# Twelve late conditioning slabs in the waits of three norms, a rebuilt LayerNorm, and the decay's low-rank product over column groups

## The chip, the cores and the metric

The kernel runs on one core of a Trainium2 chip. Its engines work side by side, each through its own program in order, and wait for one another on semaphores: TensorE (PE for its matmuls, PEld for its weight loads), VectorE (DVE), ScalarE (ACT), GpSimd (POOL) and SyncE (SP). POOL, SP and ACT also issue DMA transfers. The metric is the device time of one execution in microseconds (us); less is better.

## The reference, cut to what matters

One step of a one-layer decoder for 512 prompt tokens and 8 sampled tokens, 520 columns in all, width 1024.

```
mod = silu(c) @ w_ada + b_ada        # 9 x 1024, and 2 x 1024 of w_ada_final
h = rms_norm(x) * (1 + sc1) + sh1;   x = x + 0.5 * gt1 * swiglu(h)            # FFN1
h = rms_norm(x) * (1 + sc2) + sh2;   z = h @ w_in                             # the mixer
ca, cb, q, k, v, r, a_lr, g_conv, g_gla = split(z)
d = depthwise_conv(ca * sigmoid(cb));  y_conv = silu(layer_norm(d)) @ w_conv_out
log_a = log_sigmoid(a_lr @ w_alpha + b_alpha) / 16                            # rank 16
o = gla(q, k, v, log_a);               y_gla = (rms_norm(o) * silu(r)) @ w_gla_out
x = x + gt2 * ((sigmoid(g_conv) * y_conv + sigmoid(g_gla) * y_gla) @ w_out)
h = rms_norm(x) * (1 + sc3) + sh3;   x = x + 0.5 * gt3 * swiglu(h)            # FFN2
y = rms_norm(x) * (1 + scf) + shf
```

## The kernel before

Activations lie feature-major: eight tiles `t` of 128 features by 520 columns. Every weight product is cut into **units**, each 128 output features, numbered through the program by `plan()`. A unit (`unit`, L548) is 48 matmuls: eight k-tiles, three products (`w_hi*h_hi`, `w_hi*h_lo`, `w_lo*h_hi`), two halves of 260 columns. SP loads raw weights for two units (1 MB) into one of two slots of `raw`; ACT casts them to `w_hi` (L962), DVE subtracts for `w_lo` (L1322). Both are done in `step(n)`, once unit n is done, for unit n + 2. Even units write PSUM `pu0`, odd ones `pu1`, and a unit waits until its bank was read (`s_evac`). `unit_pair` (L564) runs two units side by side, k-tile by k-tile, as the tiles of h arrive.

**Conditioning slabs.** `w_ada` and `w_ada_final` are read in 44 slabs of 256 columns. A slab is eight fp32 matmuls with a 32-column stationary operand `c_f`, four of them in different column groups of the array (`ada_rows_of`, L581), then a copy of the rows by ACT (`ada_rows`, L985), two transposes with `sel` (`ada_transpose`, L592) and an add by DVE (`ada_out`, L1359). Slabs 0 to 7 stand at the start, 8 to 41 in pairs between the units of FFN1, 42 and 43 after it. FFN1 and FFN2 have the same 68 units, in three groups of up and down.

**A norm** (`norm_sums`, `rstd`, `modulate`): the squares of eight tiles are added up on DVE, PE sums over features with `ones` (L599), ACT takes Ln and Exp, DVE refines the root and multiplies, ACT modulates and casts, DVE subtracts for `h_lo` (L1468).

**Low rank of the decay** (`alr`, L1133): one whole unit whose first 16 output rows are used; its plan numbers stand for four units, and ACT and DVE pass two of them by counting semaphores.

**LayerNorm of the convolution** (L903 to L918): mean by PE, `centered` tiles (L1851), squares by ACT (L996) added up by DVE (L1380), `norm_sums(2)`, `o_sums` (L918) of heads 0 and 1 before the first unit of `yconv` and of heads 2 and 3 before its third (all single units); `o_roots`, `o_rstd`, and the gating of `o` (L1908 to L1913) go between the units of `yconv`. The units `ygla` read `o_hi` and `o_lo`.

Of the kernel before, what the change touches and what calls it, by code (L numbers as in the profile page):

```python
# [1968 lines left out]
```

## Time and profile before

| | |
|---|---|
| median of 3 runs | 1552.81 us (1550.1 to 1555.76) |
| the profiled execution | 1552.72 us, its span 1551.1 us |
| granted clock of TensorE, mean | 0.966 |
| FFN1, from its first unit to its last | 30.3 to 470.9 us |
| norm, then convolution, q and k, v | 470.9 to 700 us |
| gates and the linear attention | 700 to 952 us |
| LayerNorm, `yconv`, `ygla`, `out` | 952 to 1128 us |
| norm, FFN2, last norm | 1128 to 1551 us |

The profile is that of one execution; its time outside the span is 1.6 us. In the rows further on a start is in us from the start of the span, `x16` counts records (an fp32 matmul leaves two, an fp32r one), and `[5.03 <-DVE h_lo L1468]` says that the engine had been idle for 5.03 us until that instruction of DVE released it. Granted clock 1.00 is 2.4 GHz, 0.50 is 1.2 GHz.

### The profile page before, as it was taken

The numbers are of one execution on the slowest core, as the hardware profiler recorded it, in microseconds if no ns is written. First come the engines' busy times: TensorE is split into PE (matmuls) and PEld (weight loads), VectorE is DVE, ScalarE is ACT, GpSimd is POOL, SyncE is SP. The second block draws the span as 40 slices with busy tenths as digits, with TensorE's granted clock in tenths as the row PEclk, the third lists the DMA queues.
The fourth block names the chain that finished last, engine by engine and source line by source line (L and its number), as shares of the span: only waits on it lengthen the run. The fifth ranks groups of instructions, "written<-read, shape, count | busy, mean of one in ns | idle before, by whom it ended". The sixth has DMA issues, their size and how long they took to land. (4 is left out here: it accounts for less than half of the span.)

```text
span 1551.1 us, 30240 instructions
## 1 busy us (share of the span) xinstructions
PE 1451.4 (94%) x11934; PEld 1399.7 (90%) x11934; DVE 825.3 (53%) x1381; ACT 487.0 (31%) x660; POOL 73.5 (5%) x108
## 2 busy tenths in 40 slices
PE   6999999999997998999998895899979999999996
PEld 5899999999997998998998895799979999999995
DVE  5323322332256685798795977775453343333345
ACT  5322122212235223433232233522252212222233
POOL 6100000000010000000000000000000000000000
PEclk9999999999999999999898998899989999999997
DMA  9754545454554223222323333322312322322311
GB/s 311 235 168 154 172 152 173 147 178 142 170 189 147 84 81 113 72 93 79 130 93 122 105 123 132 137 83 88 103 55 82 104 85 82 108 82 84 99 61 55
DMA packets 134277, 189.03 MB, mean 122 GB/s; under 512 B 3516, under 2 KB 114512, under 8 KB 134159
## 3 DMA queue, kind: packets, MB, share of 16 engines
q1 hardware_dynamic: 113436, 114.57, 23.3%
q0 software_dynamic: 16704, 64.75, 12.5%
q10 hardware_dynamic: 4050, 8.53, 1.5%
q8 instruction: 58, 0.95, 0.3%
q14 instruction: 29, 0.23, 0.0%
HBM read 174.37 MB, written 14.41 MB: 122 GB/s over the span
## 5 line engine op out<-in xcount | busy, mean ns | idle before, releaser
L1322 DVE TENSOR_TENSOR w_lo<-raw,w_hi 128x1024 fp32r<-128x1024 f32 x218 | 266.8, 1225 | 589.6 <-ACT w_hi L962 589.4
L548 PE MATMUL pu<-h_hi,w_hi 128*128 128x260 f32 x2480 | 508.1, 286 | 19.4 <-DVE w_lo L1322 10.5
L548 PE MATMUL pu<-h_hi,w_lo 128*128 128x260 f32 x2480 | 501.5, 284 | 0.0
L548 PE MATMUL pu<-h_lo,w_hi 128*128 128x260 f32 x2480 | 500.8, 284 | 0.0
L962 ACT CAST w_hi<-raw 128x1024 fp32r<-128x1024 f32 x218 | 227.9, 1046 | 682.3 <-PE pu L548 670.6
L548 PEld LDWEIGHTS pu<-h_hi,w_hi 128*128 128x128 f32 x2480 | 384.5, 190 | 27.5 <-issue 10.9
L548 PEld LDWEIGHTS pu<-h_lo,w_hi 128*128 128x128 f32 x2480 | 384.4, 190 | 0.0
L548 PEld LDWEIGHTS pu<-h_hi,w_lo 128*128 128x128 f32 x2480 | 384.3, 189 | 0.0
L1617 DVE SCALAR_TENSOR_TENSOR d<-u,cw,d 128x512 f32<-128x512 f32 x240 | 162.9, 747 | 0.0
L548 PE MATMUL pu<-f_hi,w_hi 128*128 128x260 f32 x704 | 143.0, 284 | 2.0 <-DVE f_lo L1571 2.0
L548 PE MATMUL pu<-f_hi,w_lo 128*128 128x260 f32 x704 | 141.8, 283 | 0.0
L548 PE MATMUL pu<-f_lo,w_hi 128*128 128x260 f32 x704 | 141.3, 282 | 0.0
L548 PEld LDWEIGHTS pu<-f_hi,w_hi 128*128 128x128 f32 x704 | 108.3, 188 | 4.9 <-issue 2.5
L548 PEld LDWEIGHTS pu<-f_hi,w_lo 128*128 128x128 f32 x704 | 108.4, 188 | 0.0
L548 PEld LDWEIGHTS pu<-f_lo,w_hi 128*128 128x128 f32 x704 | 108.3, 188 | 0.0
L1088 ACT CAST f_hi<-sg 128x520 f32 (+1 forms) x44 | 27.6, 627 | 87.8 <-DVE sg L1568 87.8
L1571 DVE TENSOR_TENSOR f_lo<-sg,f_hi 128x520 f32 (+1 forms) x44 | 30.8, 701 | 40.4 <-ACT f_hi L1088 40.4
L581 PE MATMUL pg<-raw_a,c_f 128*32 128x256 f32 x640 | 38.9, 382 | 1.1 <-DMA raw_a<-in_w_ada 1.1
L1207 ACT ACTIVATE work<-work 128x512 f32<-128x512 f32 x28 | 17.7, 632 | 68.2 <-DVE work L1724 68.0
L418 POOL DMA_DIRECT2D raw_a<-in_w_ada x28 | 24.6, 884 | 297.6 <-PE pg L581 296.8
L811 PEld LDWEIGHTS pg<-work 128*128 128x128 f32 x224 | 28.0, 196 | 8.6 <-DVE work L1743 4.4
L811 PE MATMUL pg<-work 128*128 128x128 f32 x224 | 31.4, 287 | 3.2 <-DVE work L1743 3.2
(260 smaller groups left out, 1242.3 us busy)
## 6 DMA issues: line engine op xcount, KB each, us to landing
raw_a<-in_w_ada POOLq DMA_DIRECT2D x32, 1024.0 KB, 7.8
raw<-in_w_in SPq DMA_DIRECT2D x30, 1024.0 KB, 5.3
raw<-in_ffn_up SPq DMA_DIRECT2D x22, 1024.0 KB, 5.3
raw<-in_ffn_gate SPq DMA_DIRECT2D x21, 1024.0 KB, 5.3
raw<-in_ffn_down SPq DMA_DIRECT2D x16, 1024.0 KB, 5.1
raw_a<-in_w_ada_final POOLq DMA_DIRECT2D x8, 1024.0 KB, 7.4
gates_d<-sg ACTq DMA_DIRECT2D x24, 260.0 KB, 2.0
raw<-in_ffn_down SPq DMA_DIRECT2D x8, 768.0 KB, 4.5
```

The source lines that it names most:

```text
L418: pool.dma_start(dst, v[:, :, bass.ds(c, 256)]).then_inc(s_loaded, 16)
L548: last = mm(pu[p][:, e, 0:HALF], w[p][:, k, :], m[:, k, e * HALF:(e + 1) * HALF], start=(k == 0 and j == 0), stop=(k == k_tiles - 1 and j ...
L581: last = mm(pg[CG * g:CG * (g + 1), 2 + slot, 0:256], c_f[:, k, :], src[:, k, :], start=(k < 4), stop=(k >= 4), tile_position=(0, CG * g))
L811: last = mm(pg[:, l % 2, c * CH:(c + 1) * CH], m, m if rhs is None else rhs[:, c * CH:(c + 1) * CH], start=True, stop=True)
L962: nc.scalar.copy(w_hi[p][:], raw[:, slot, :, p * P:(p + 1) * P]).then_inc(s_hi, 1)
L1088: nc.scalar.copy(tile(f_hi, Lin(2 * k0 + c - 2, 2, i).value()), sg[:, c - 2, :]).then_inc(s_ahi, 1)
L1207: af(E_[:, l % 2, :], E_[:, l % 2, :], ACT.Exp, scale=1 / 16).then_inc(s_ge, 1)
L1322: V.tensor_tensor(w_lo[p][:], raw[:, slot, :, p * P:(p + 1) * P], w_hi[p][:].bitcast(F32), ALU.subtract).then_inc(s_lo, 1)
L1571: V.tensor_tensor(tile(f_lo, t.value()), s, tile(f_hi, t.value()).bitcast(F32), ALU.subtract).then_inc(s_a, 1)
L1617: conv.mark(V.scalar_tensor_tensor(d[:, t, 0:NP], flat(u[:, t:t + 1, bass.ds(tap + s, NP)]), cw[:, bass.ds((tap + s) * KT + t, 1)], d[:, t ...
```

## The change

1. **Slabs.** Slabs 32 to 43 leave FFN1 and the place behind it. Four each stand in the norm before the mixer, in the LayerNorm, and in the norm before FFN2 (`late_slabs`), two to a PSUM bank, with one copy of 512 columns for two slabs (`late_rows`), eight transposes for four (`late_transposes`) and one add (`late_out`). Their loads, issued by POOL, go to the memory that `LATE` names.
2. **LayerNorm.** PE sums each tile's squares itself; DVE no longer adds them up. The mean's sum no longer waits for `s_oe`. The first head's sums and root stand before `yconv`, whose first two units are now a `unit_pair`; the other heads follow between the units. `refine_d` replaces `refine`.
3. **Decay's low rank.** `alr` is gone from the plan. `a_rows` multiplies h by `wa` (16 columns of `w_in`, padded to 32) in column groups, into PSUM bank `pg`; `walpha` holds its 16 rows four times, 128 partitions with zeros between, so that the next product adds up the groups.

```diff
+LATE0 = 32
+LATE_BANK = [0, 2, 0]
-                        + [("conv", 16), ("alr", 4), ("qk", 8), ("v", 8), ("gates", 24),
+                        + [("conv", 16), ("qk", 8), ("v", 8), ("gates", 24),
...
+        LATE = [((raw_a, "a1"), (raw_q, "q")), ((raw_v, "v2"), (raw_h, "h")), ((raw_a, "a3"), (raw_v, "v3"))]
...
             ffn(1)
+            sp.wait_ge(s_wz, 1)
+            sp.dma_start(wa[:, :, 0:RANK], w_in[:, W_IN["a"]:W_IN["a"] + RANK].rearrange("(k p) n -> p k n", p=P)
+                         ).then_inc(s_wa, 16)
...
-            pair(Lin(at["alr"]), w_in, W_IN["a"], (w_in, W_IN["a"]))
...
+            late_load(0, 1)
+            pool.wait_ge(s_ad, LATE0)
+            late_load(0, 0)
...
+                if h + 1 == HEADS:
+                    pool.wait_ge(s_gk, HEADS)
+                    late_load(1, 0)
                 pool.wait_ge(s_oe, 2 * h + 1)
                 pool.dma_start(st_out[h], ST).then_inc(s_sto, 16)
+                if h + 1 == HEADS:
+                    pool.wait_ge(s_done, at["yconv"])
+                    late_load(1, 1)
...
+            pool.wait_ge(s_done, at["out"])
+            late_load(2, 0)
+            late_load(2, 1)
...
+            def late_slabs(stage):
+                for two in range(2):
+                    src, name = LATE[stage][two]
+                    pe.wait_ge(s_late[name], 32)
+                    for j in range(2):
+                        last = slab_rows(src[:, j], 2 + two, 256 * j)
+                    last.then_inc(s_lb, 1)
...
-            ada(Lin(ADA_SLABS - 2))
-            ada(Lin(ADA_SLABS - 1))
+            pe.wait_ge(s_ar, LATE0)
+            late_slabs(0)
...
-            pe.wait_ge(s_evac[1], n // 2)
-            unit(Lin(n), 0, h_hi, h_lo, done=4)
+            def a_rows():
+                pe.wait_ge(s_wa, 16)
+                pe.wait_ge(s_cve, KT)
+                for r in range(2):
+                    for j, m in enumerate((h_hi, h_lo)):
+                        for e in range(2):
+                            for g in range(4):
+                                last = mm(pg[CG * g:CG * (g + 1), 2 + e, 0:HALF], wa[:, 4 * r + g, :],
+                                          m[:, 4 * r + g, e * HALF:(e + 1) * HALF].bitcast(F32), start=(r == 0 and j == 0),
+                                          stop=(r == 1 and j == 1), tile_position=(0, CG * g))
+                last.then_inc(s_ao, 1)
...
             pe.wait_ge(s_ln, 2)
+            sums(sg[:, 2, :]).then_inc(s_ss, 1)
             pe.wait_ge(s_oe, 2 * HEADS)
-            sums(sg[:, 2, :]).then_inc(s_ss, 1)
-            norm_sums(2)
+            late_slabs(1)
+            for t in range(KT):
+                pe.wait_ge(s_sq, KT + t + 1)
+                sums(sg[:, t % 3, :], start=(t == 0), stop=(t == KT - 1)).then_inc(s_sqf, 1)
...
+            pe.wait_ge(s_lr, 4)
+            o_sums(0)
+            unit_pair(Lin(at["yconv"]), h_hi, h_lo, s_h, 2 * KT)
+            o_sums(1)
+            late_transposes(1)
+            for c in range(2, 4):
+                unit(Lin(at["yconv"] + c), c % 2, h_hi, h_lo)
+                o_sums(c)
...
             norm_sums(3)
+            pe.wait_ge(s_or, HEADS)
+            late_slabs(2)
...
-            rstd(4, SILU)
+            rstd(3, SILU)
+            late_rows(2, 0)
             modulate(3, SC3, SH3)
+            late_rows(2, 1)
...
             modulate(3, SC3, SH3)
+            late_out(2)
```

TensorE's program between the last unit of the convolution (fed by `h_hi`, `h_lo`, L548 before and L580 after) and the transposes of `u`; first of before, the first rows of `alr` only:

```order
L548 MATMUL pu<-h_lo,w_hi 128x260 x2
L548 MATMUL pu<-h_hi,w_lo 128x260 x2
L114 REGISTER_ALU
L114 COMPARE_AND_BRANCH
L548 MATMUL pu<-h_hi,w_hi 128x260 x2
L548 MATMUL pu<-h_lo,w_hi 128x260 x2
L548 MATMUL pu<-h_hi,w_lo 128x260 x2
L548 MATMUL pu<-h_hi,w_hi 128x260 x2
```

and after:

```order
L580 MATMUL pu<-h_lo,w_hi 128x260 x2
L580 MATMUL pu<-h_hi,w_lo 128x260 x2
L114 REGISTER_ALU
L114 COMPARE_AND_BRANCH
L814 MATMUL pg<-h_hi,wa 32x260 x8
L814 MATMUL pg<-h_lo,wa 32x260 x8
L814 MATMUL pg<-h_hi,wa 32x260 x8
L814 MATMUL pg<-h_lo,wa 32x260 x8
L580 MATMUL pu<-h_hi,w_hi 128x260 x2
L580 MATMUL pu<-h_lo,w_hi 128x260 x2
```

The loop's end is followed by 32 matmuls into `pg` where the 48 of the unit `alr` stood; the unit of q comes next in both.

TensorE's program in the LayerNorm, from the end of the attention's loop (L873 and L943 are its last products) to the first unit of `yconv`, before:

```order
L873 MATMUL pg<-work 128x128
L876 REGISTER_ALU
L876 COMPARE_AND_BRANCH
L599 MATMUL pg<-sg,ones 128x260 x6
L918 MATMUL pg<-work,ones 128x260 x8
L548 MATMUL pu<-h_hi,w_hi 128x260 x2
```

and after:

```order
L943 MATMUL pg<-work 128x128
L946 REGISTER_ALU
L946 COMPARE_AND_BRANCH
L657 MATMUL pg<-sg,ones 128x260 x2
L617 MATMUL pg<-raw_v,c_f 32x256 x16
L617 MATMUL pg<-raw_h,c_f 32x256 x16
L657 MATMUL pg<-sg,ones 128x260 x16
L995 MATMUL pg<-work,ones 128x260 x4
L596 MATMUL pu<-h_hi,w_hi 128x260 x2
```

The mean's two matmuls are followed by four slabs; the sums of squares are sixteen matmuls instead of four; of the heads' sums one head is left in front (four matmuls of eight), and the first rows of `yconv` are those of a pair (L596).

DVE's program behind the last `h_lo` of the LayerNorm, where the heads' roots and the first units of `yconv` are served, before:

```order
L1400 TENSOR_TENSOR lb<-lb,sg 128x520 [waits dve_step]
L1890 TENSOR_SCALAR vt<-vt 128x8
L1322 TENSOR_TENSOR w_lo<-raw,w_hi 128x1024 [waits raw1_loaded,unit_done,w_hi_ready,gate_reloaded_gc,dve_step]
L1884 SCALAR_TENSOR_TENSOR work<-work,pu 128x520
L1322 TENSOR_TENSOR w_lo<-raw,w_hi 128x1024 [waits w_hi_ready,raw1_loaded,unit_done]
L1884 SCALAR_TENSOR_TENSOR work<-work,pu 128x520
L1397 TENSOR_TENSOR sg<-lb 128x520 [waits o_rstd_ready,o_root_ready]
```

and after:

```order
L1497 SCALAR_TENSOR_TENSOR lb<-sg,lb 128x520 [waits dve_step]
L1418 TENSOR_TENSOR w_lo<-raw,w_hi 128x1024 [waits raw1_loaded,w_hi_ready,unit_done,gate_reloaded_gc]
L1972 SCALAR_TENSOR_TENSOR work<-work,pu 128x520
L1418 TENSOR_TENSOR w_lo<-raw,w_hi 128x1024 [waits w_hi_ready,raw1_loaded,unit_done]
L1972 SCALAR_TENSOR_TENSOR work<-work,pu 128x520
L1464 TENSOR_TENSOR mod<-pg,vt 128x80 [waits late_rows_transposed]
L1495 SCALAR_TENSOR_TENSOR sg<-pg,lb 128x520 [waits o_rstd_ready,o_root_ready]
```

Before, two heads' roots stand ahead of the first `w_lo`; after, one does, and the late slabs' add and the second head's root stand behind the second unit's read.

## Rows read from the trace of the kernel before

**Rows 1.** The page, busy time of each engine over the span.

```profile
PE 1451.4 (94%) x11934; PEld 1399.7 (90%) x11934; DVE 825.3 (53%) x1381; ACT 487.0 (31%) x660; POOL 73.5 (5%) x108
```

**Rows 2.** Six stretches: length, busy PE, PEld, DVE, ACT, POOL, granted clock, DMA share, GB/s.

```profile
350.00:400.00 50.00, 50.00 (x451) 47.87 (x450) 14.23 (x19) 13.09 (x19) 3.52 (x4) 1.00 0.53 169
484.00:487.00 3.00, 3.00 (x15) 3.00 (x15) 2.77 (x5) 2.82 (x5) 0.00 (x0) 0.50 0.00 0
593.00:595.00 2.00, 1.77 (x8) 1.78 (x9) 2.00 (x4) 0.00 (x0) 0.00 (x0) 0.50 1.09 383
700.00:750.00 50.00, 46.59 (x339) 43.97 (x338) 45.97 (x83) 18.88 (x28) 0.58 (x1) 0.93 0.28 88
966.00:970.00 4.00, 3.41 (x8) 2.53 (x8) 0.54 (x1) 0.40 (x1) 0.00 (x0) 0.50 0.02 4
1350.00:1450.00 100.00, 100.00 (x835) 100.00 (x834) 36.61 (x60) 24.29 (x28) 0.00 (x0) 1.00 0.30 95
```

**Rows 3.** Timeline of TensorE in the last group of FFN1 (start, us).

```profile
455.06 1.93 PE L581 MATMUL pg<-raw_a,c_f 128*32 128x256 f32 x32
...
456.92 0.51 PE L548 MATMUL pu<-f_hi,w_hi 128*128 128x260 f32 x2
...
465.62 0.95 PE L592 MATMUL pg<-sel,lb 128*128 128x10 f32 x8
...
466.43 0.48 PE L548 MATMUL pu<-f_hi,w_hi 128*128 128x260 f32 x2
```

**Rows 4.** Timeline of the norm between FFN1 and the mixer.

```profile
474.06 1.93 PE L581 MATMUL pg<-raw_a,c_f 128*32 128x256 f32 x32
...
478.56 0.81 ACT L1011 ACTIVATE sg<-sg,mod 128x512 f32<-128x512 f32 x1 [1.07 <-DVE sg L1450]
...
481.02 0.77 PE L564 MATMUL pu<-h_hi,w_hi 128*128 128x260 f32 x2 [5.03 <-DVE h_lo L1468]
...
495.32 0.95 PE L592 MATMUL pg<-sel,lb 128*128 128x10 f32 x8
...
498.58 0.47 PE L548 MATMUL pu<-h_hi,w_hi 128*128 128x260 f32 x2 [2.31 <-DVE w_lo L1322]
```

**Rows 5.** Timeline of the norm before FFN2.

```profile
1137.85 0.77 PE L564 MATMUL pu<-h_hi,w_hi 128*128 128x260 f32 x2 [6.88 <-DVE h_lo L1468]
```

**Rows 6.** Timeline around the unit of the decay's low rank.

```profile
584.13 0.51 PE L548 MATMUL pu<-h_hi,w_hi 128*128 128x260 f32 x2 [3.00 <-DVE u L1629]
...
593.23 0.80 PE L548 MATMUL pu<-h_hi,w_hi 128*128 128x260 f32 x2 [3.09 <-DVE w_lo L1322]
...
600.48 1.03 PE L756 MATMUL pg<-ident,u 128*38 128x128 f32 x8
```

**Rows 7.** Timeline of the LayerNorm and the units behind it.

```profile
953.52 1.11 PE L599 MATMUL pg<-sg,ones 128*128 128x260 f32 x4 [1.27 <-ACT qk L1244]
...
954.69 3.95 ACT L1252 ACTIVATE work<-qk 128x1040 f32<-128x1040 f32 x4
...
966.59 3.84 PE L599 MATMUL pg<-sg,ones 128*128 128x260 f32 x8 [11.96 <-DVEq L1385]
...
974.80 0.82 ACT L1259 ACTIVATE d<-d,vt 128x520 f32<-128x520 f32 x1 [1.67 <-DVE d L1854]
...
985.98 0.70 DVE L1872 TENSOR_TENSOR h_lo<-d,h_hi 128x520 fp32r<-128x520 f32 x1 [0.68 <-ACT h_hi L1262]
...
1022.02 0.48 PE L548 MATMUL pu<-h_hi,w_hi 128*128 128x260 f32 x2 [1.61 <-DVE work L1884]
```

**Rows 8.** The chain of work that ended last: start, us, what.

```profile
993.49 3.72 PE pg L918 x16
...
1038.95 0.71 DVE o_lo L1913
```

**Rows 9.** DMA issues (KB each, us to landing): whole span, then 975 to 1010 us.

```profile
raw_a<-in_w_ada POOLq DMA_DIRECT2D x32, 1024.0 KB, 7.8
...
raw<-in_w_conv_out SPq DMA_DIRECT2D x1, 1024.0 KB, 11.6
```

More of the change, by code:

```diff
@@ L686, in ada_part @@
                 def ada_part(c, m, i):
-                    if which == 1:
+                    if which == 1 and m < LATE0:
                         if m == ADA0 and i is None and c == 2:
@@ L985, in ada_rows, with late_rows @@
                 nc.scalar.copy(rows_a[:, slot], pg[:, 2 + slot, 0:256]).then_inc(s_ar, 1)
+            def late_rows(stage, two):
+                act.wait_ge(s_lb, 2 * stage + two + 1)
+                nc.scalar.copy(rows_l[:, two], pg[:, 2 + two, :]).then_inc(s_lr, 1)
             def psum(p):
@@ L1068, in ada_part @@
                 def ada_part(c, m, i):
-                    if which == 1 and c % 4 == 0:
+                    if which == 1 and m < LATE0 and c % 4 == 0:
                         ada_rows(Lin(m + c // 2, 2, i))
@@ L1129, in _ @@
                 conv_units(i, at["conv"] + 4, 4)
-            n = at["alr"]
-            act.wait_ge(s_done, n + 1)
-            for e in (1, 0):
-                nc.scalar.copy(alr[:, e * HALF:(e + 1) * HALF], pu[0][0:RANK, e, 0:HALF]).then_inc(s_evac[e], 2)
-            for c in range(2):
-                act.wait_ge(s_raw[1], Lin(n).half().half().value(16, 16))
-                act.sem_inc(s_hi, 1)
-            for c in range(2, 4):
-                act.wait_ge(s_lo, n + c + 1)
-                step(Lin(n + c))
+            act.wait_ge(s_ao, 1)
+            nc.scalar.copy(halves(alr), pg[:, 2:4, 0:HALF]).then_inc(s_alr, 1)
             def z_out(h):
@@ L1262, in _, with o_high @@
                 nc.scalar.copy(h_hi[:, t, :], d[:, t, :]).then_inc(s_hh, 1)
[L1264 to L1287 removed]
+            o_squares(1)
+            for c in range(2):
+                step(Lin(at["yconv"] + c))
+            o_squares(2)
+            o_squares(3)
+            act.preload_act_table_set(LN_EXP)
+            o_root(1)
+            def o_high(t):
+                act.wait_ge(s_of, t.value(add=1))
+                nc.scalar.copy(tile(o_hi, t.value()), tile(qk, t.value())).then_inc(s_oh, 1)
+            o_high(Lin(0))
+            o_high(Lin(1))
+            for c in range(2, 4):
+                step(Lin(at["yconv"] + c))
+                o_root(c)
+                o_high(Lin(c))
+            with act.Fori(0, 1) as i:
+                for c in range(4):
+                    t = Lin(4 + c, 4, i)
+                    step(t + at["yconv"])
+                    o_high(t)
             with act.Fori(0, 2) as i:
@@ L1549, in ada_part @@
                 def ada_part(c, m, i):
-                    if which == 1 and c % 4 == 2:
+                    if which == 1 and m < LATE0 and c % 4 == 2:
                         ada_out(Lin(m + c // 2 - 1, 2, i))
@@ L1600, in _ @@
             modulate(1, SC2, SH2)
-            ada_out(Lin(ADA_SLABS - 2))
-            ada_out(Lin(ADA_SLABS - 1))
+            late_out(0)
             chain.link(V.memset(u[:, :, 0:TAPS - 1], 0.0))
@@ L1642, in _ @@
             conv.end(3)
[L1643 to L1649 removed]
             def sample_conv():
[L1653 to L1654 removed]
+                dve.wait_ge(s_evac[0], at["qk"] // 2)
+                dve.wait_ge(s_evac[1], at["qk"] // 2)
                 dve.wait_ge(s_cve, KT)
@@ L1886, in _, with o_low @@
+            def o_low(t):
+                dve.wait_ge(s_oh, t.value(add=1))
+                V.tensor_tensor(tile(o_lo, t.value()), tile(qk, t.value()), tile(o_hi, t.value()).bitcast(F32),
+                                ALU.subtract).then_inc(s_osp, 1)
+            gn = vt[:, VROW["gla_norm"]:VROW["gla_norm"] + KT]
+            chain.link(V.tensor_scalar(gn, gn, -0.25 / DV, None, ALU.mult))
             o_rstd(0)
+            dve.wait_ge(s_gr["gc"], 16)
+            yconv_unit(Lin(0))
+            yconv_unit(Lin(1))
@@ L1887, in _ @@
+            late_out(1)
             o_rstd(1)
[L1889 to L1914 removed]
@@ new lines, in _ @@
+            dve.wait_ge(s_or, 2)
+            dve.wait_ge(s_gr["r"], 16)
+            o_gated(Lin(0), 0)
+            o_gated(Lin(1), 0)
+            yconv_unit(Lin(2))
+            o_low(Lin(0))
+            o_low(Lin(1))
+            o_gated(Lin(2), 1)
+            o_rstd(2)
+            yconv_unit(Lin(3))
+            o_low(Lin(2))
+            o_gated(Lin(3), 1)
+            o_rstd(3)
+            dve.wait_ge(s_or, HEADS)
+            with dve.Fori(0, 1) as i:
+                for c in range(4):
+                    t = Lin(4 + c, 4, i)
+                    yconv_unit(t)
+                    o_low(t + (-1))
+                    o_gated(t, 2 + c // 2)
```

205 lines of the change are left out of this document (99 added, 106 removed).

## The prediction

> **What bounds the kernel now.** I read the page first: TensorE is busy in 94% of the span, no other engine in more than 53% [rows 1]. So the time is TensorE's stream plus its waits. Then the busy time by stretch [rows 2]: in FFN1 and in FFN2 TensorE is busy throughout. FFN2 gives the price of a unit: 835 matmuls in 100 us, 0.1198 us each, 5.75 us for 48. In FFN1 only 451 matmul records stand in 50 us; slabs fill the rest. In the attention VectorE is busy in 46 of 50 us and TensorE waits a little; there the two go in step. Then I read the timeline at each place the diff touches, for what TensorE waits for: 5.03 us in the first norm and 6.88 us in the norm before FFN2 [rows 4, 5], 3.00 and 3.09 us around the low-rank unit [rows 6], 11.96 us in the LayerNorm [rows 7]. Last the chain that ended last, which from 966 to 1040 us runs through the LayerNorm and the gating of `o` [rows 8].
>
> **Slabs out of FFN1.** A pair of slabs takes from 455.06 to 456.92, 1.86 us, and its transposes from 465.62 to 466.43, 0.81 us [rows 3]; the first record of each also starts about 0.09 us later than a matmul in step would. That is 2.7 us a pair. Five of the pairs (32 to 41) leave a stretch where TensorE never waits: **-13.5 us**. FFN2 runs the same units without slabs and without idle time, so the units left behind are not slowed by their weight casts.
>
> **The first norm.** Two slabs stand in it now; four will, from 474.06 to about 477.9. ScalarE modulates the first tile at 478.56 after 1.07 us idle, and TensorE starts at 481.02 [rows 4]. The first bank is full at 476.0, its copy (0.65 us) fits ahead of 478.56, and the second copy comes after the last tile. So the slabs cost nothing while the wait is there; without it 1.9 us. The transposes for four slabs, instead of two, stand at 495.32 and take 1.6 instead of 0.8 us; behind them VectorE adds, clears two buffers and makes the `w_lo` for which TensorE waits until 498.58 [rows 4]. With one add instead of two: **+0.6 us**.
>
> **The norm before FFN2.** Four slabs, 3.8 us, fit into 6.88 [rows 5]. The transposes behind the pair of units lie in a wait for `w_lo` as above, 2.3 us; but `late_out` stands ahead of that `w_lo` on VectorE and waits for the transposes, so `w_lo` comes later: **+0.9 us**. Between 0 and 1.8.
>
> **The decay's low rank.** Now TensorE waits 3.00 us for `pu1`, runs the unit, waits 3.09 us for `w_lo`, and the unit of q then runs from 593.23 to 600.48, 7.25 us instead of 5.75, its first part at granted clock 0.50 [rows 2, 6]. After, `a_rows` writes `pg` and starts at once at 581.1 (584.13 less 3.00). It is 32 fp32 matmuls in column groups, as the slabs are, 64 records of 260 columns: 2 x 1.86 x 260/256 + 0.1 = 3.9 us. The weights of the first two q units are made in the last steps of the convolution, so q starts at 585.0 and ends at 590.8: **-9.7 us**. Its bank was read by 584.1. All behind follows in the order of the programs: VectorE's next work is q's `w_lo` after the first unit of q, so it moves by the same, although it is 92% busy afterwards [rows 2]. Bounds: 4.8 us if only the two waits but one and the clock go (TensorE's 1.9 us less work, 3.09 idle, and no more), and 9.7.
> The rule for packing in the Trainium skill, "TensorE: Matmul & The Clock Gate", Part 3, Measured speedup vs the span model, gives a factor of 3.07 for four row tiles, which would make `a_rows` about 5.0 us (estimate) and this term -8.6. The slabs here run four column groups at close to four times the rate of single matmuls: 32 records in 1.86 us against 16 in 3.72 [rows 3, 8]. I take the rows.
>
> The load of `wa`, 1024 pieces of 64 bytes, stands on SP's queue behind FFN1's last load. No row has such pieces. A 1 MB load has as many pieces, so I take its landing, 5.3 us without traffic and 11.6 beside another (raw loads [rows 9]), as the upper bound; it is needed 100 us later, and the next raw load is issued some 9 us later. Cost 0 to 3 us, I take 0.
>
> **The LayerNorm.** Followed step by step with the durations of the same instructions:
> - The mean's sums start at 952.4 instead of 953.52 [rows 7]. The slabs follow: 953.5 to 957.4, if the second pair has landed. It is issued at 945.4, two loads, and a pair of slabs lands 7.8 us after issue [rows 9]: 954 to 955, beside 1 MB of state stored. Up to 2 us late in the bad case.
> - ScalarE squares one head instead of four: 955.75 instead of 958.6 (954.69 + 3.95 [rows 7]). Squares need 0.64 us a tile, TensorE's sums of a tile 0.96 (four records of 0.24). TensorE limits: 957.4 + 7.7 = 965.1. Now its sums end at 970.43, at clock 0.50 [rows 2, 7].
> - From there to the first SiLU was 4.4 us (974.80). Now ScalarE also roots head 0 behind the sums of head 0 (967.05) and then loads its table: 967.05 + 0.69 + 0.64 + 1.28 = 969.7. So -5.1 us. The eight tiles take what they took, the last `h_lo` ends at 981.6 instead of 986.68.
> - TensorE idles from 967.05 to 972.0, 4.9 us, and will start at 1.2 GHz. The pair of units is 96 matmuls, 11.5 us, plus 1.4 to 2.6 us of slow clock: done at about 985.4. Two units were done at 993.4 [rows 8]: -8 us.
> - Then `o_sums(1)` and the transposes, 3.5 us, while `w_lo` is made; the third unit starts at 988.9 instead of 997.2. Two heads' sums (1.93 us each) now stand between the units, which costs 3.9 us, and the waits of 1.61 us at 1022.02 [rows 7] and before `ygla` shrink. VectorE's order is the limit at the end: roots 2.2, `w_lo` 1.2, read 0.6, gating 1.4, `o_lo` 0.7 us, each behind the engine it waits for. I get the last `o_lo` at 1034.5 instead of 1039.65 [rows 8]: **-5.1 us**. Bounds: 0, if VectorE's and ScalarE's handoffs eat it, and 8.3, if `ygla` never waits.
>
> **The clock.** The idle time before the first tile falls from 5.03 to about 3.1 us in the first norm, and from 6.88 to about 3.0 before FFN2. The rows stand on both sides of that: after 3.00 us TensorE ran on at 2.4 GHz (0.51 us for two, then 0.24), after 3.09 at 1.2 GHz [rows 2, 6]. At 484 to 487 it still ran at 0.50: 15 matmuls where 25 would be [rows 2]. Staying warm is worth 2.8 us in the first norm (the pair then ends 1.44 us behind the last tile) and 2.2 before FFN2, no more, as the tiles come each 1.46 us. I take one of the two: **-2.4 us**.
> The Trainium skill ("TensorE: Matmul & The Clock Gate", Part 1, What's actually happening) has the gate fall after idle time and look freely, not from the last matmul on. By that either norm may fall on either side from run to run, which the two rows bear out; cold at both, the sum is 2.4 us higher.
>
> **Sum.** -13.5 + 0.6 + 0.9 - 9.7 - 5.1 - 2.4 = -29.2 us. From the profiled execution's 1552.7 us: **1523.5 us**. The median of the three runs shown is 1552.8, the same within 0.1.
>
> **Rivals.**
> - *Some step in the LayerNorm is given back* (chance 0.15): the second pair of slabs lands late, or `o_sums` between units and VectorE's longer order hold `ygla` at 1039. For it: VectorE is busy in most of that stretch, and four engines hand over per tile. Against: 11.96 us of wait are there to take. 1523.5 + 5.1 = 1528.6 us.
> - *The low rank gives half* (0.10): `a_rows` at the price of unpacked matmuls (64 x 0.24 = 15.4 us) is excluded by the slabs, but VectorE, which paces the attention, could absorb some: 1523.5 + 4.9 = 1528.4, with the former 1533.5.
> - *More than forecast* (0.12): both norms warm, and `yconv`'s pair warm, with `ygla` waiting less: 1523.5 - 2.6 - 3.2 = 1517.7.
> - *The slabs' loads cost more than the slabs* (0.02, the other sign). Four loads at the start of `out`, 4 MB, stand beside SP's raw loads; one raw load beside 2 MB landed in 11.6 instead of 5.3 us [rows 9]. A load has about 14.7 us from its issue to its cast (three units less 2.5). A stall of s us there makes the change slower once s passes 29 + 5 = 34 us, when the time would be over 1557; 4 MB at the same rate bring 6 to 12 us more landing, a stall of 3 at most.
> - *The slabs in the norms cost what they cost in FFN1* (0.03): then -13.5 shrinks by the 10 slabs' 9.3 us, 1532.8. Against it: the waits are in the rows.
>
> **How the numbers follow.** The forecast's case has 0.58; its own range is 1519 to 1528 (clock 2.6 either way, `late_out` and `wa` up to 3 more). The range over all, with the bounds of the low rank and of the LayerNorm singly: 1516 to 1532 us; outside remain both losses together and what I have not seen. About 0.3% (4.7 us) is what a measurement of this kernel can tell from no change. Every case but the other sign's lies 19 us or more below 1552.8: faster 0.95, within 0.3% 0.03, slower 0.02.
>
> **What would show it.** FFN1 from first to last unit 13 to 14 us shorter. The first matmul of the first norm's pair at the same distance from the norm's sums, 5.9 us behind their end. No idle time before `a_rows`, which takes 3.9 us, and none before q. In the LayerNorm sums at 2.4 GHz right behind the slabs; first SiLU about 17 us behind the mean's sums instead of 21. The first `ygla` unit done 5 us less behind them. Wrong it would be if TensorE waits for the slabs' loads, if ScalarE's copies hold a norm's tiles, or if VectorE's idle time in `yconv` vanishes.

## The result, and the profile after

The changed kernel takes 1533.68 us (median of 4 runs, 1532.07 to 1534.01), the kernel before 1554.28 us beside it. The ratio is 0.9865, 95% interval 0.9841 to 0.9890: 21 us less (17 to 25), where 29 us less and 1523.5 us were forecast, and the range ended at 1532. The profiled execution took 1534.01 us, its span is 1531.3 us, 19.8 us less than before.

The page of the changed kernel: busy time by engine, and the chain that ended last, by line. It answers to [rows 1].

```profile
PE 1445.2 (94%) x11974; PEld 1395.4 (91%) x11974; DVE 817.1 (53%) x1362; ACT 483.0 (32%) x651; POOL 75.8 (5%) x112
...
PE pu L580 45%; PE pu L596 3%; DVE d L1714 1%; DVE w_lo L1418 1%; DMA raw_h<-in_w_ada_final 1%; ACT w_hi L1045 1%; PE pg L657 1%; DVE work L1833 1%; DVE work L1842 1%; PE pg L941 1%; PE pg L881 1%; DVE work L1826 0%; PE pg L995 0%; DVE sg L1547 0%; DVE work L1814 0%
```

1% of the span is a transfer, `raw_h`, which the prediction held to land in time. TensorE's timeline of the changed kernel shows where (start us, duration, line, output<-inputs, in brackets the idle time ahead and who ended it):

```profile
460.75 1.93 PE L617 MATMUL pg<-raw_a,c_f 128*32 128x256 f32 x32
...
467.71 0.77 PE L596 MATMUL pu<-h_hi,w_hi 128*128 128x260 f32 x2 [3.30 <-DVE h_lo L1565]
...
480.77 1.85 PE L639 MATMUL pg<-sel,lb 128*128 128x10 f32 x16
485.06 0.77 PE L580 MATMUL pu<-h_hi,w_hi 128*128 128x260 f32 x2 [2.44 <-issue]
...
568.97 1.09 PE L814 MATMUL pg<-h_hi,wa 128*32 128x260 f32 x16
...
578.45 1.03 PE L826 MATMUL pg<-ident,u 128*38 128x128 f32 x8
...
927.36 1.14 PE L657 MATMUL pg<-sg,ones 128*128 128x260 f32 x4 [0.44 <-DVE sg L1936]
928.44 1.93 PE L617 MATMUL pg<-raw_v,c_f 128*32 128x256 f32 x32
937.20 3.64 PE L617 MATMUL pg<-raw_h,c_f 128*32 128x256 f32 x32 [6.83 <-DMA raw_h<-in_w_ada_final]
940.77 7.93 PE L657 MATMUL pg<-sg,ones 128*128 128x260 f32 x32
948.54 1.92 PE L995 MATMUL pg<-work,ones 128*128 128x260 f32 x8
...
968.61 1.91 PE L995 MATMUL pg<-work,ones 128*128 128x260 f32 x8
...
1115.41 0.48 PE L596 MATMUL pu<-h_hi,w_hi 128*128 128x260 f32 x2 [3.31 <-DVE h_lo L1565]
...
1128.48 1.85 PE L639 MATMUL pg<-sel,lb 128*128 128x10 f32 x16
1132.12 0.51 PE L580 MATMUL pu<-h_hi,w_hi 128*128 128x260 f32 x2 [1.78 <-DVE w_lo L1418]
```

ScalarE's first SiLU and VectorE's last `o_lo`, which answer to [rows 7, 8]:

```profile
953.17 0.82 ACT L1354 ACTIVATE d<-d,vt 128x520 f32<-128x520 f32 x1
...
1016.18 0.70 DVE L1985 TENSOR_TENSOR o_lo<-qk,o_hi 128x520 fp32r<-128x520 f32 x1 [0.69 <-ACT o_hi L1369]
```

Read as a ledger, each place against the same place before. The last columns say how far ahead of before the changed kernel stands, and what the stretch up to there gave.

| place (before, after) | ahead by | the stretch gave | forecast |
|---|---|---|---|
| first tile of the first norm (481.02, 467.71) | 13.3 | 13.3 | 13.5 |
| unit behind the transposes (498.58, 485.06) | 13.5 | 0.2 | -0.6, +2.4 for the clock here or before FFN2 |
| low rank starts (581.1, 568.97) | 12.1 | -1.4 | 0 |
| first unit of q done (600.48, 578.45) | 22.0 | 9.9 | 9.7 |
| mean's sums (953.52, 927.36) | 26.2 | 4.1 | 1.1 |
| last `o_lo` (1038.95, 1016.18) | 22.8 | -3.4 | 4.0 |
| first tile before FFN2 (1137.85, 1115.41) | 22.4 | -0.3 | 0 |
| unit behind the transposes there (1153.41, 1132.12) | 21.3 | -1.2 | -0.9 |
| end of the span (1551.1, 1531.3) | 19.8 | -1.5 | 0 |

Four rows are off: the LayerNorm by 7.4 us, the stretches behind both transposes by 1.4 and 1.5 us, and the attention by 3 us the other way. Look at the clock for the last three. First the kernel before, three stretches (length, busy PE, PEld, DVE, ACT, POOL, granted clock, DMA share, GB/s) and the row of its 1153.41, then the changed kernel at the same places:

```profile
498.50:508.50 10.00, 9.92 (x84) 9.95 (x85) 2.94 (x3) 2.09 (x5) 0.00 (x0) 1.00 0.34 107
887.40:893.40 6.00, 5.93 (x29) 5.93 (x29) 2.56 (x4) 0.00 (x0) 0.00 (x0) 0.51 0.96 335
1153.40:1163.40 10.00, 9.99 (x83) 9.99 (x84) 3.18 (x4) 2.32 (x4) 0.00 (x0) 1.00 0.35 107
```

```profile
1153.41 0.51 PE L548 MATMUL pu<-h_hi,w_hi 128*128 128x260 f32 x2 [1.77 <-DVE w_lo L1322]
```

```profile
485.00:495.00 10.00, 9.94 (x72) 9.97 (x73) 2.41 (x3) 2.09 (x5) 0.00 (x0) 0.84 0.33 107
865.10:868.40 3.30, 3.24 (x29) 3.25 (x30) 2.54 (x4) 0.00 (x0) 0.00 (x0) 1.00 0.91 280
1132.00:1142.00 10.00, 9.88 (x69) 9.89 (x70) 2.41 (x4) 1.05 (x1) 0.00 (x0) 0.83 0.33 105
```

Behind the transposes the kernel before ran at 2.4 GHz (84 and 83 matmuls in 10 us), the changed one partly at 1.2 GHz (72 and 69): 12 matmuls of 0.12 us are 1.4 us. In the attention it is the kernel before that fell: the same 29 records of `prompt_o` took 6.0 us there and 3.3 here, behind the same wait (2.40 us before, 2.38 after). The change doesn't touch them. But one head is not the whole account: the first head's `prompt_o` went the other way, 5.01 us before and 6.08 after (762.67 and 738.47), and the four together took 21.2 and 19.2 us. What settles it is the same stretch in other traces. From q's unit done to the mean's sums it is 353.0 us in the kernel before and 349.4 in `a_rows_alone`, whose attention is the same but for the semaphores that announce the low rank; and in six kernels that have the changed kernel's program there (itself, `load_first`, `late_out_behind`, `late_out_only`, `warm_norms`, `warm_short`) it is 347.9 to 351.7. Single executions differ by 3.6 to 3.8 us in this stretch with nothing changed, so the 3 us are no effect of the change that these traces could show.

### The profile page after: what moved, and what is told of

The parts are those of the page before. It is cut to its first block, busy times and chain, and to the rows that moved or that the text cites. A ratio compares the mean times of both kernels' runs of the same rounds, so it can differ in the third digit from the quotient of the medians.

```text
span 1531.3 us, 30166 instructions
## 1 busy us (share of the span) xinstructions
PE 1445.2 (94%) x11974; PEld 1395.4 (91%) x11974; DVE 817.1 (53%) x1362; ACT 483.0 (32%) x651; POOL 75.8 (5%) x112
## 3 DMA queue, kind: packets, MB, share of 16 engines
q0 software_dynamic: 16800, 64.85, 12.7%
## 4 chain that ended last, share of the span: by engine, by line
PE 53%; DVE 9%; issue 4%; ACT 2%; DMA 1%; DVEq 1%; POOL 0%; ACTq 0%
PE pu L580 45%; PE pu L596 3%; DVE d L1714 1%; DVE w_lo L1418 1%; DMA raw_h<-in_w_ada_final 1%; ACT w_hi L1045 1%; PE pg L657 1%; DVE work L1833 1%; DVE work L1842 1%; PE pg L941 1%; PE pg L881 1%; DVE work L1826 0%; PE pg L995 0%; DVE sg L1547 0%; DVE work L1814 0%
## 5 line engine op out<-in xcount | busy, mean ns | idle before, releaser
L580 PE MATMUL pu<-h_hi,w_hi 128*128 128x260 f32 x2432 | 497.7, 286 | 12.3 <-issue 6.5
L580 PE MATMUL pu<-h_hi,w_lo 128*128 128x260 f32 x2432 | 492.4, 284 | 0.0
L580 PE MATMUL pu<-h_lo,w_hi 128*128 128x260 f32 x2432 | 491.3, 284 | 0.0
L580 PEld LDWEIGHTS pu<-h_hi,w_hi 128*128 128x128 f32 x2432 | 377.6, 190 | 17.7 <-issue 10.5
L580 PEld LDWEIGHTS pu<-h_hi,w_lo 128*128 128x128 f32 x2432 | 377.3, 190 | 0.0
L580 PEld LDWEIGHTS pu<-h_lo,w_hi 128*128 128x128 f32 x2432 | 376.7, 189 | 0.0
L580 PE MATMUL pu<-f_hi,w_hi 128*128 128x260 f32 x704 | 142.6, 284 | 2.0 <-DVE f_lo L1669 2.0
L580 PE MATMUL pu<-f_hi,w_lo 128*128 128x260 f32 x704 | 141.8, 283 | 0.0
L580 PE MATMUL pu<-f_lo,w_hi 128*128 128x260 f32 x704 | 141.3, 282 | 0.0
L580 PEld LDWEIGHTS pu<-f_hi,w_hi 128*128 128x128 f32 x704 | 108.3, 188 | 4.1 <-DVE f_lo L1669 2.5
L580 PEld LDWEIGHTS pu<-f_hi,w_lo 128*128 128x128 f32 x704 | 108.4, 188 | 0.0
L580 PEld LDWEIGHTS pu<-f_lo,w_hi 128*128 128x128 f32 x704 | 108.3, 188 | 0.0
L596 PE MATMUL pu<-h_hi,w_hi 128*128 128x260 f32 x128 | 29.0, 312 | 11.7 <-DVE h_lo L1565 6.6
L596 PEld LDWEIGHTS pu<-h_hi,w_hi 128*128 128x128 f32 x128 | 22.2, 212 | 13.3 <-issue 13.0
```

What stands on the lines that cost most here:

```text
L580: last = mm(pu[p][:, e, 0:HALF], w[p][:, k, :], m[:, k, e * HALF:(e + 1) * HALF], start=(k == 0 and j == 0), stop=(k == k_tiles - 1 and j ...
L596: last = mm(pu[p][:, e, 0:HALF], w[p][:, k, :], m[:, k, e * HALF:(e + 1) * HALF], start=(k == 0 and j == 0), stop=(k == KT - 1 and j == 2))
```

## Experiments: one part at a time

**`a_rows_alone`**, the kernel before with this part only:

```
-  pe.wait_ge(s_evac[1], n // 2)
-  unit(Lin(n), 0, h_hi, h_lo, done=4)
...
+  a_rows()
```

> The kernel before with one part of the change: the decay's low rank by a_rows in column groups, in place of the whole unit alr. Theory of the prediction: the two waits around the unit (3.00 and 3.09 us), 1.9 us of its work and the slow start of q go, 9.7 us less than the kernel before. Rival: VectorE, which paces the attention, gives half of it back, 4.8 us less. In the profile the q unit should start 3.7 to 3.9 us behind a_rows, without a wait; what counts is how far the sums of the LayerNorm's mean stand ahead of 953.52.

Measured: ratio 0.9930 (0.9918 to 0.9942), 10.9 us less (9.0 to 12.7). `a_rows` starts at 581.20, and q's unit is done at 590.68, 9.8 us earlier than before [rows 6]. The row behind it is `u_tails`, as there:

```profile
581.20 1.09 PE L764 MATMUL pg<-h_hi,wa 128*32 128x260 f32 x16
...
590.68 1.03 PE L776 MATMUL pg<-ident,u 128*38 128x128 f32 x8
```

VectorE gave nothing back: the mean's sums stand at 940.09, 13.4 us ahead. That is 3.6 us more than the part itself gave, the spread of the attention named above, and this profile is of the fastest of six runs. The interval is the safer ground: it begins at 9.0 us, and the rival said 4.8. The rival is out.

**`ln_alone`**, the kernel before with the rebuilt LayerNorm only (cut to TensorE's order of the sums):

```
+  sums(sg[:, 2, :]).then_inc(s_ss, 1)
   pe.wait_ge(s_oe, 2 * HEADS)
-  sums(sg[:, 2, :]).then_inc(s_ss, 1)
-  norm_sums(2)
+  for t in range(KT):
+      pe.wait_ge(s_sq, KT + t + 1)
+      sums(sg[:, t % 3, :], start=(t == 0), stop=(t == KT - 1)).then_inc(s_sqf, 1)
```

> The kernel before with one part of the change: the rebuilt LayerNorm with its order of the heads of o, without slabs in it. Theory of the prediction: 5.1 us less than the kernel before (bounds 0 and 8.3), as the mean's sums start 1.1 us earlier and the last o_lo stands about 4 us nearer to them. Rival, after the result: the rebuilt order is what costs, VectorE and ScalarE hand over too often, and the kernel takes as long as before or up to 3.4 us more, which is what the profile of the change shows between the mean's sums and the first unit of ygla.

Measured: ratio 0.9965 (0.9952 to 0.9978), 5.4 us less (3.4 to 7.5), where 5.1 was the prediction's term. The mean's sums start at 952.57 and `ygla` at 1034.10, 81.5 us behind them. So the rebuilt order isn't what costs in the changed kernel, where that distance is 89.6 us (927.36 to 1016.94).

**`both_no_slabs`**, both parts, the slabs where they were:

```
-            late_slabs(1)
...
-            late_transposes(1)
...
-            late_out(1)
```

(and likewise for stages 0 and 2; slabs 8 to 41 go between the units of FFN1 again, 42 and 43 into the first norm).

> Both of these parts, and the slabs as in the kernel before. If the parts add up, 14 to 16 us less than the kernel before. What the change then has beyond it is the price of the moved slabs: by the prediction 12 to 14 us less again, by the profile of the change (13.5 saved in FFN1, 8.5 lost to a load in the LayerNorm, about 1.5 lost in each of two norms) some 2 to 6 us less.

Measured: ratio 0.9882 (0.9868 to 0.9897), 18.3 us less (16.0 to 20.5). The parts add up (10.9 + 5.4 = 16.3, within the intervals). The whole change has 0.9865: moving twelve slabs brought some 3 us by the ratios, and as the two intervals overlap it may be nothing. The forecast had 12 us for the slabs and 2.4 for the clock.

## Experiments: where the slabs' gain went

**`load_first`**, on GpSimd's queue:

```
                 late_load(1, 0)
+                pool.wait_ge(s_done, at["yconv"])
+                late_load(1, 1)
             pool.wait_ge(s_oe, 2 * h + 1)
             pool.dma_start(st_out[h], ST).then_inc(s_sto, 16)
-            if h + 1 == HEADS:
-                pool.wait_ge(s_done, at["yconv"])
-                late_load(1, 1)
```

> The changed kernel, with the two loads of raw_h for the slabs in the LayerNorm issued ahead of the store of the last head's state on GpSimd's queue (and ahead of its wait for o) instead of behind it. Theory: that store, and the wait ahead of it, are why the slabs' load lands at 937.2; now it is issued at about 915 and lands before 928, the wait of 6.83 us goes and so do 1.7 us of slow clock in the slabs behind it: 8.5 us less than the changed kernel, about 1525. Rival A: the memory's rate is the limit, with SyncE's load of raw weights beside it; the load then still lands near 933 and about half comes back, 4 us. Rival B: the wait only moves, to a load of SyncE or to the gates read back behind the store, and nothing comes back.

Measured: ratio 0.9816 (0.9804 to 0.9829), 1525.31 us: 7.6 us less than the changed kernel by the ratios. GpSimd's timeline, first of the changed kernel, then of this one:

```profile
919.58 0.90 POOL L531 DMA_DIRECT2D out_gla_s<-work  x1 [22.95 <-ACT qk L1320]
920.47 1.75 POOL L493 DMA_DIRECT2D raw_h<-in_w_ada_final  x2
```

```profile
916.28 1.76 POOL L493 DMA_DIRECT2D raw_h<-in_w_ada_final  x2 [18.74 <-PE pu L579]
920.35 0.89 POOL L533 DMA_DIRECT2D out_gla_s<-work  x1 [2.30 <-ACT qk L1319]
```

DMA issues of the changed kernel from 919 to 938 us (KB each, median us to landing), and of this one from 914 to 932:

```profile
raw_h<-in_w_ada_final POOLq DMA_DIRECT2D x2, 1024.0 KB, 14.4
out_gla_s<-work POOLq DMA_DIRECT2D x1, 1024.0 KB, 6.7
raw<-in_w_conv_out SPq DMA_DIRECT2D x1, 1024.0 KB, 13.4
```

```profile
raw_h<-in_w_ada_final POOLq DMA_DIRECT2D x2, 1024.0 KB, 7.9
out_gla_s<-work POOLq DMA_DIRECT2D x1, 1024.0 KB, 9.7
```

The load was issued only 4.2 us earlier and landed 6.5 us faster, with the store's 1 MB no longer ahead of it. The two transfers that TensorE waits for landed 12.9 and 15.8 us after issue in the changed kernel, 6.5 and 9.2 us here. Why the store costs so much isn't separated: it may be the place in line on the queue, or the memory's rate. The four megabytes (store, two loads, SyncE's raw weights) had all landed 17.6 us after the first issue in the changed kernel and 16.2 us here, at 316 and 323 GB/s over 921 to 937 us and 918 to 932 us, so nearly all that changed is who landed first. TensorE, with no wait ahead of the second pair of slabs:

```profile
929.36 1.93 PE L616 MATMUL pg<-raw_v,c_f 128*32 128x256 f32 x32
931.11 1.91 PE L616 MATMUL pg<-raw_h,c_f 128*32 128x256 f32 x32
932.95 7.28 PE L656 MATMUL pg<-sg,ones 128*128 128x260 f32 x32
```

The slabs of `raw_h` take 1.91 us here and 3.64 behind the wait; the wait of 6.83 and 1.7 us of slow clock are 8.5 us. Rivals A and B are out as they were put: the load did not land near 933 but at 926.4, and no wait took the place of the old one.

**`late_out_behind`**, `load_first` with VectorE's two `late_out` behind a `w_lo` (the wait for `s_mod` in the first norm moves to the state's transposes, and VectorE's first round of FFN2's loop is written out to have a place for it):

```
-            late_out(2)
             ffn(2, GT3)
...
                             step(n)
+                            if which == 2 and g == 0 and i is None and c == 1:
+                                late_out(2)
```

> The kernel load_first with VectorE's late_out of the first norm and of the norm before FFN2 behind the w_lo for which TensorE waits, instead of ahead of it. The prediction gave this place 0.9 us in the norm before FFN2 (bounds 0 and 1.8); the profile of the change shows 16.71 us from the first tile's matmul to the third unit instead of 15.56, and 1.2 us is what should come back there, and 0.5 to 1 us in the first norm, in all about 2 us less than load_first. Rival: the transposes alone (1.85 us) fill the wait, and 0.2 us or nothing comes back.

Measured: ratio 0.9761 (0.9737 to 0.9786), 1517.38 us: about 8 us less than `load_first` (7.9 by the medians, 8.5 by the ratios), four times what was expected. VectorE's timeline before FFN2, changed kernel first:

```profile
1130.44 0.24 DVE L1464 TENSOR_TENSOR mod<-pg,vt 128x80 f32<-128x80 f32 x1 [4.94 <-PE pg L639]
1130.83 2.36 DVE L1418 TENSOR_TENSOR w_lo<-raw,w_hi 128x1024 fp32r<-128x1024 f32 x2 [0.15 <-issue]
```

```profile
1117.54 1.23 DVE L1418 TENSOR_TENSOR w_lo<-raw,w_hi 128x1024 fp32r<-128x1024 f32 x1 [2.40 <-ACT w_hi L1045]
```

TensorE in this kernel, behind the pair of either norm:

```profile
480.08 1.85 PE L638 MATMUL pg<-sel,lb 128*128 128x10 f32 x16
482.03 0.51 PE L579 MATMUL pu<-h_hi,w_hi 128*128 128x260 f32 x2
...
1116.79 1.85 PE L638 MATMUL pg<-sel,lb 128*128 128x10 f32 x16
1118.82 0.51 PE L579 MATMUL pu<-h_hi,w_hi 128*128 128x260 f32 x2 [0.18 <-DVE w_lo L1418]
```

`w_lo` follows `w_hi` at once and no longer waits for the transposes. From the transposes to the next unit it is 1.95 us instead of 4.29 in the first norm (2.3 saved) and 2.03 instead of 3.64 before FFN2 (1.6 saved). And the clock no longer falls behind them (84 and 83 matmuls in the next 10 us, where `load_first` has 72 and 70), which is worth another 1.4 and 1.5 us: 6.8 us in all. In this run the pair before FFN2 also stayed at 2.4 GHz (1.3 us); the same wait of 3.30 us was followed by 1.2 GHz in `load_first` and `late_out_only`, so that part is put down to chance.

**`late_out_only`**, the same edit on the changed kernel, without `load_first`:

```
-            late_out(2)
             ffn(2, GT3)
```

> The changed kernel with only the place of late_out moved behind the first w_lo in both norms; the loads of raw_h stay behind the store. If this edit's 8 us (late_out_behind against load_first, ratio 0.9761 against 0.9816) are its own and not the chip's, the ratio to the kernel before is 0.9865 less 0.0055, 0.981, about 1525. Rival: part of those 8 us was the clock's chance, and the ratio is 0.983 to 0.985.

Measured: ratio 0.9818 (0.9793 to 0.9843), 0.0047 below the changed kernel. By the ratios the edit is worth about 7 us by itself, though its interval just touches the changed kernel's (0.9841 to 0.9890). The trace agrees: 1.95 and 2.03 us from the transposes to the next unit, and 84 and 83 matmuls behind them. It and the load add up (7 and 8 us, 16 together).

**`warm_norms`**, `load_first` with filling matmuls that write a PSUM bank that the next unit clears:

```
+            def keep_warm(count, dst):
+                for _ in range(count):
+                    mm(dst, ones[:], c_flat, start=True, stop=True)
...
                 for p in range(2):
                     weights_and_psum(n + p, p)
+                keep_warm(fill, pu[0][:, 0, 0:256])
```

> The kernel load_first with matmuls that nobody reads (ones by c_f, 256 columns, 0.24 us each) in TensorE's waits: 12 ahead of the first tile's pair of units in the first norm and in the norm before FFN2, 18 in the LayerNorm, 8 and 6 behind the transposes of the two norms. Theory: each of these five places is followed by a stretch at granted clock 0.50, about 3.4 us, in which a matmul takes 0.217 instead of 0.120 us; it is the wait ahead that brings it, and without it up to 1.6 us a place come back, 5 to 8 us in all. Rival A: the clock falls all the same, and nothing comes back. Rival B: the tiles come every 1.4 us and the pairs wait for them anyway, so that only the two places behind the transposes and part of the others pay: 3 us.

Measured: ratio 0.9816 (0.9790 to 0.9841), the same as `load_first`. The clock did what the theory said, but the fill was sized wrongly. The row of the fill and the pair behind it:

```profile
464.43 5.45 PE L588 MATMUL pu<-c_f,ones 128*128 128x256 f32 x24
469.52 0.59 PE L603 MATMUL pu<-h_hi,w_hi 128*128 128x260 f32 x2
```

12 of these matmuls are 24 records and take 5.45 us, not 2.9: an fp32 matmul stands as two records of 0.23 us. It overran the wait of 3.30 us, and the first tile's matmul came 1.8 us late; the pair, at 2.4 GHz, then took 11.65 us instead of 13.07, a gain of 1.4. **`warm_all`** had the same fault in the attention:

```
+                pe.wait_ge(s_evac[0], nxt.half().value())
+                keep_warm(9, pu[0][:, 0, 0:256])
                 pe.wait_ge(s_gp, h.value(8, 8))
```

> The kernel warm_norms with nine such matmuls more for each head ahead of prompt_o, where TensorE waits 2.4 to 3.35 us for VectorE. Theory: the slow stretches of the attention (some 17 us at 0.50 in load_first) go, and where TensorE is the later one behind them time comes back, 2 to 5 us less than warm_norms. Rival: VectorE paces the attention, and the time stays as that of warm_norms within 1 us.

Measured: 0.9807 (0.9781 to 0.9833), 1524.77 us: the same as `warm_norms` within 1 us, as the rival said. The clock did hold, all four `prompt_o` took 3.29 us without a wait ahead of them, but from q's unit to the mean's sums it is 352.3 us where `warm_norms` has 347.9.

**`warm_short`**, `late_out_behind` with 6, 10 and 6 fills (first norm, LayerNorm, before FFN2) and none behind the transposes:

```
-  unit_pair(Lin(at["yconv"]), h_hi, h_lo, s_h, 2 * KT)
+  unit_pair(Lin(at["yconv"]), h_hi, h_lo, s_h, 2 * KT, fill=10)
```

> The kernel late_out_behind with filling matmuls of the right length: in warm_norms 12 took 5.45 us where 3.3 us were free, so that the first tile's matmul came 1.8 us late and took back what the clock gave. Here 6 stand ahead of the pair in each of the two norms (2.8 us) and 10 in the LayerNorm (4.6 us in 5.07). Theory: the pairs then run in 11.7 us from the first matmul to the transposes, as the one pair of late_out_behind did that stayed at 2.4 GHz, instead of 13.1 us, in all three places: up to 1.3 us each, 2.6 to 4 us less than late_out_behind. Rival: the short fill leaves the clock to fall in half of the cases, or the tiles limit the pairs, and the time is the same within 1 us.

Measured: ratio 0.9735 (0.9712 to 0.9757), 1513.49 us, 4 us less than `late_out_behind` by the medians and by the ratios. The intervals of the ratios overlap, the times don't (1512.3 to 1514.75 against 1514.81 to 1519.11, measured beside a kernel before of 1556.2 and 1553.0 us). First norm:

```profile
463.57 2.86 PE L588 MATMUL pu<-c_f,ones 128*128 128x256 f32 x12
466.85 0.51 PE L603 MATMUL pu<-h_hi,w_hi 128*128 128x260 f32 x2 [0.42 <-DVE h_lo L1574]
...
478.68 1.85 PE L646 MATMUL pg<-sel,lb 128*128 128x10 f32 x16
```

The transposes start 11.83 us behind the first tile's matmul, where the changed kernel needed 13.06 (467.71 to 480.77).

**`warm_short_all`**, the same with four fills ahead of each `prompt_o`:

```
+                keep_warm(4, pu[0][:, 0, 0:256])
                 pe.wait_ge(s_gp, h.value(8, 8))
```

> The kernel warm_short with four such matmuls more for each head ahead of prompt_o (1.85 us of the 2.4 to 3.35 us in which TensorE waits for VectorE). Theory: the slow stretches behind prompt_o, 3 to 7 us each, become shorter, and 1 to 4 us come back. Rival: VectorE paces the attention and nothing comes back; in warm_all, with nine, the attention took 4.5 us longer than in warm_norms.

Measured: ratio 0.9711 (0.9689 to 0.9733), 1509.82 us (1509.57 to 1510.49), the fastest, 24 us below the changed kernel. That is 3.7 us less than `warm_short` beside it; the ratios' intervals overlap, the times don't. From the start of `a_rows` to the mean's sums it is 355.65 us (564.10 to 919.75), in the six kernels without fills in the attention 357.4 to 361.2 (`warm_norms` the least). The four `prompt_o` took 13.5 us together, 20.1 in `warm_short`. Only part of these 6.6 us shortened the stretch, which fits VectorE as its pace, with TensorE the later one in some places while at 1.2 GHz; no run shows in which. One head's fill, from the timeline:

```profile
789.28 1.97 PE L588 MATMUL pu<-c_f,ones 128*128 128x256 f32 x8
792.78 0.71 PE L952 MATMUL pg<-work 128*128 128x128 f32 x4 [1.52 <-DVE work L1847]
```

## Why the prediction was wrong, point by point

- **Slabs out of FFN1, -13.5 us**: right. 13.3 us ahead at the first norm's first tile.
- **The first norm, +0.6 us**: the slabs and copies fitted, as forecast; the first tile waits 3.30 us. That the stretch gained 0.2 us is two things that cancel: from the transposes to the next unit it took 4.29 us instead of 3.27 (+1.0, where 0.6 was forecast), and the pair ahead of them 13.06 instead of 14.29 (-1.2), which belongs to the clock's term. Nothing was put down for the clock behind the transposes, and it cost 1.4 us.
- **The norm before FFN2, +0.9 us**: the ledger's 1.2 looks as if it lay within the bounds of 0 and 1.8, but that is luck. From the pair's end to the next unit it took 3.64 us instead of 1.77, +1.9, above the upper bound, and the pair was 0.7 us shorter by the clock. Again a slow stretch behind it, 1.5 us.
- **The low rank, -9.7 us**: right. 9.9 us in the profile, 10.9 (9.0 to 12.7) alone. The lower bound of 4.8 was added up wrongly: 1.9 and 3.09 are 5.0.
- **The load of `wa`, 0**: nothing waited for it.
- **The LayerNorm, -5.1 us**: the working was right in all but one line. From the end of the squares' sums to the first SiLU, the two units done and the last `o_lo` it took 4.6, 20.1 and 68.3 us (948.54 to 953.17, 968.61 and 1016.88); forecast were 4.6, 20.3 and 69.4. Alone the part gave 5.4 us. The failed step is the second pair's load: "a pair of slabs lands 7.8 us after issue [rows 9]: 954 to 955, beside 1 MB of state stored. Up to 2 us late in the bad case". It landed 14.4 us after issue by the median of the two, 937.2, and TensorE waited 6.83 us and then ran the slabs at half clock. The 7.8 us was the median over FFN1, where no store stands ahead on the queue; here 1 MB of store was issued 0.9 us ahead on the same queue, and raw weights came in beside. That store I named, and priced at 2 us at most. This is the rival "some step in the LayerNorm is given back" by its first mechanism, with a price of 8.5 us where I had 5.1.
- **The clock, -2.4 us**: the second step that failed. Ahead of the pairs it did much of what was forecast, in another way. Neither norm stayed warm: the first fell at once (0.77 at 467.71), the one before FFN2 0.8 us behind its first matmul. But behind the shorter waits (3.30 and 3.31 us instead of 5.03 and 6.88) the clock came back sooner. Three us behind the first tile's matmul the kernel before still ran at 0.50, 15 matmuls in 3 us [rows 2], and the changed kernel had 25:

```profile
470.70:473.70 3.00, 3.00 (x25) 3.00 (x25) 2.76 (x5) 2.82 (x5) 0.00 (x0) 0.94 0.02 5
```

That gave 1.2 and 0.7 us, 1.9 of the 2.4. Part of it may be chance: with the old waits the pairs took 13.6 to 13.9 us in the first norm and 13.0 to 14.3 before FFN2 in `a_rows_alone`, `ln_alone` and `both_no_slabs`. What I had not counted is the clock behind the transposes, where it fell in both norms and cost 2.9 us. In the changed kernel and in `load_first` 1.85 us of transposes with ten columns each and 2.44 or 1.78 us of wait behind them were followed by half clock all four times; in the four kernels with the same transposes and a wait of 0.2 us or less behind them (`late_out_behind`, `late_out_only`, `warm_short`, `warm_short_all`) none of eight was. With the shorter transposes of the kernel before it can go either way: behind the same 2.31 us the clock held in three traces, and fell in `both_no_slabs` (two rows, then the stretch behind them):

```profile
494.72 0.95 PE L600 MATMUL pg<-sel,lb 128*128 128x10 f32 x8
497.99 0.47 PE L556 MATMUL pu<-h_hi,w_hi 128*128 128x260 f32 x2 [2.31 <-DVE w_lo L1354]
...
498.00:508.00 10.00, 10.00 (x72) 10.00 (x73) 2.33 (x3) 2.09 (x5) 0.00 (x0) 0.83 0.33 107
```

The Trainium skill ("TensorE: Matmul & The Clock Gate", Part 1, What's actually happening) has the gate look freely at what TensorE did; by that the same wait can end on either side. The runs fit it: behind the same wait of 3.30 us before FFN2 the pair took 11.74 us in `late_out_behind` (1105.05 to 1116.79) and 13.07 in `late_out_only` (1113.09 to 1126.16), and in the attention `prompt_o` took 6.0 and 3.3 us behind 2.40 and 2.38.
- **Sum.** Forecast -29.2. The load with its clock +8.5; the clock behind the transposes +2.9; the clock ahead of the pairs +0.5 (1.9 gained of 2.4); the longer transposes and the place of `late_out` +1.4 (2.9 instead of 1.5); the LayerNorm's rest -1.1; the attention -3.0 beyond the 1.1 forecast, which is that execution's; all other terms together +0.3: -19.7, and the span is 19.8 shorter. With `load_first` the kernel takes 1525.31 us, 1.8 above the forecast. That closeness is partly luck: the clock's 2.9 us are still in it, and the attention's 3.0 stand against them.
- **The range** ended at 1532 and the time was 1533.7. It took in the low rank's and the LayerNorm's bounds singly, but 2 us at most for this load, though the rows had one raw load landing in 11.6 us instead of 5.3 beside 2 MB [rows 9]. Its ends were not built alike either: the lower is 1519 less the LayerNorm's 3.2, and in the same way the upper would have been 1528 and 5.1, 1533. Part of the miss is the kernel before, 1554.3 us beside the changed one where the forecast started at 1552.7; by the ratio the changed kernel is at 1531.7.

What stays open: why the clock falls behind one wait and not behind the same wait of another run was not controlled, only avoided. Whether the load was late by its place in line or by the memory's rate isn't separated. And the attention's 3.0 us rest on single executions that differ by as much with nothing changed there; the medians, which know nothing of it, agree with the other terms within their intervals.

## What to carry to other kernels

A transfer's landing time from another stage is worth nothing until you have read what is issued just ahead of it and beside it at the new place: issue the load ahead of the store, if its buffer is free. A step that is put in front of work on a waiting engine's supplier (`late_out` ahead of `w_lo`) costs the time until its own input comes, here 1.6 to 2.3 us for an instruction of 0.24, and the clock behind it. Fill a wait of TensorE with work, but measure one filling instruction first and stay shorter than the wait: 5.45 us in a wait of 3.3 took back what the clock gave, 2.86 us brought 4 us over three places.

## What the runs showed of the hardware

- Two loads of 1 MB issued right behind a 1 MB store on GpSimd's queue, with 1 MB of raw weights beside them, landed 12.9 and 15.8 us after issue, and 6.5 and 9.2 us when issued ahead of it; the store then took 9.7 instead of 6.7 us and the raw weights 10.8 instead of 13.4. The bytes moved at about the same rate in both (316 and 323 GB/s).
- Transposes with ten output columns, 16 records in 1.85 us, followed by 1.8 to 2.4 us of idle time, were followed by a stretch at half clock (72 and 69 matmuls in 10 us instead of 84) in the changed kernel and in `load_first`; with at most 0.2 us of idle time they weren't, in eight places of four kernels. 8 records in 0.95 us and 2.31 us of idle time were followed by it in one trace of four.
- An fp32 matmul of a full 128x128 stationary by 256 columns stands as two records and took 0.45 us (12 in 5.45), about four of the 0.12 us records of fp32r.
